# Alternating PSUM bank sets for the last down projection, and a sum of squares placed before its last quarter

## The reference

```python
h = rmsnorm(x, norm2_g[l])
u = causal_dwconv(jnp.einsum('bsd,df->bsf', h, ffn_up[l]), ffn_conv[l])
u_gate, u_val = jnp.split(u, 2, axis=-1)
x = x + jnp.einsum('bsf,fd->bsd', jax.nn.silu(u_gate) * u_val, ffn_down[l])
return rmsnorm(x, final_g)
```

## Time and profile before

| what | value |
|---|---|
| time, median of 3 executions | 2527.88 us |
| lowest and highest of the 3 | 2523.84 and 2528.88 us |
| profiled execution, its own time | 2525.59 us |
| profiled execution, its span (first to last instruction) | 2523.8 us |
| mean granted TensorE clock in it | 0.991 of full |
| TensorE busy with matmuls | 2456.4 us, 97% |
| VectorE busy | 1813.6 us, 72% |
| ScalarE busy | 1141.6 us, 45% |

### The profile page before, as it was taken

The page is one execution under the profiler, slowest core; times in us unless marked ns, Lnnn a source line. Parts: engine busy times, 40 slices in busy tenths (PEclk is TensorE's granted clock), DMA queues, the critical chain, the costliest instruction groups (busy, mean ns, idle before and its releaser), DMA issues.

```text
span 2523.8 us, 35020 instructions
## 1 busy us (share of the span) xinstructions
PE 2456.4 (97%) x13048; PEld 2062.8 (82%) x13048; DVE 1813.6 (72%) x2964; ACT 1141.6 (45%) x2080; POOL 0.3 (0%) x6
## 2 busy tenths in 40 slices
PE   8999999999998989999999999999999999999996
PEld 5888888777887657887888888888888888888884
DVE  6676666533344665338788888888888888888885
ACT  5444443323233444225555555555555555555542
POOL 0000000000000000000000000000000000000000
PEclk9999999999999989999999999999999999999998
DMA  4421112212325124213233333333333333333331
GB/s 170 151 71 52 69 54 71 83 64 108 109 85 210 42 100 151 94 61 120 89 101 101 101 103 112 109 106 110 102 102 108 101 101 101 105 101 101 101 121 67
DMA packets 72635, 252.82 MB, mean 100 GB/s; under 512 B 10112, under 2 KB 10240, under 8 KB 60716
## 3 DMA queue, kind: packets, MB, share of 16 engines
q1 hardware_dynamic: 72492, 250.91, 29.9%
HBM read 242.97 MB, written 13.15 MB: 101 GB/s over the span
## 4 chain that ended last, share of the span: by engine, by line
PE 54%; DVE 1%; issue 0%; ACT 0%; DVEq 0%; ACTq 0%
PE bank L1797 19%; PE bank L1778 15%; PE bank L1783 10%; PE bank L1758 4%; PE bank L1782 3%; PE bank L1781 3%; DVE x_t L2336 0%; DVE x_t L2327 0%; PE bank L2153 0%; DVE rms_row L2333 0%; ACT w_hi_far L1590 0%; DVE x_t L1957 0%; PE bank L2150 0%; PE bank L1765 0%; ACT rms_row L2255 0%
## 5 line engine op out<-in xcount | busy, mean ns | idle before, releaser
L1590 ACT ACTIVATE w_hi_far<-w_raw_far 128x512 fp32r<-128x512 f32 x768 | 484.1, 631 | 581.4 <-PE bank L1783 243.8
L1596 DVE TENSOR_TENSOR w_lo_far<-w_raw_far,w_hi_far 128x512 fp32r<-128x512 f32 x768 | 521.0, 688 | 165.2 <-ACT w_hi_far L1590 161.2
L1783 PE MATMUL bank<-y_parts,w_lo_far 128*128 128x256 f32 x2240 | 626.8, 280 | 0.0
L1778 PE MATMUL bank<-y_parts,w_hi_far 128*128 128x512 f32 x1600 | 565.8, 393 | 0.0
L233 PE MATMUL bank<-h_hi,w_hi 128*128 128x512 f32 x1120 | 471.7, 421 | 13.7 <-DVE w_lo L193 9.6
L1797 PE MATMUL bank<-ffn_g,w_hi_far 128*128 128x512 f32 x1408 | 466.9, 393 | 7.7 <-DVE x_t L2327 7.5
L233 PE MATMUL bank<-h_lo,w_hi 128*128 128x512 f32 x1120 | 440.6, 393 | 0.0
L233 PE MATMUL bank<-h_hi,w_lo 128*128 128x512 f32 x1120 | 439.8, 393 | 0.0
L1783 PEld LDWEIGHTS bank<-y_parts,w_lo_far 128*128 128x128 f32 x2240 | 421.6, 188 | 6.4
L1778 PEld LDWEIGHTS bank<-y_parts,w_hi_far 128*128 128x128 f32 x1600 | 300.4, 188 | 65.5
L193 DVE TENSOR_TENSOR w_lo<-w_raw,w_hi 128x512 fp32r<-128x512 f32 x312 | 203.7, 686 | 168.3 <-ACT w_hi L184 167.4
(11 more groups left out here) (309 smaller groups left out, 2657.6 us busy)
## 6 DMA issues: line engine op xcount, KB each, us to landing
w_raw_far<-in_ffn SPq DMA_DIRECT2D x167, 512.0 KB, 3.9
w_raw<-in_weights SPq DMA_DIRECT2D x77, 1024.0 KB, 5.0
w_raw_far<-in_ffn SPq DMA_DIRECT2D x162, 256.0 KB, 3.8
w_raw_far<-in_weights SPq DMA_DIRECT2D x8, 1024.0 KB, 4.9
x_t<-in_x_t SPq DMA_DIRECT2D x7, 1024.0 KB, 9.9
bias_rows<-bias_row SPq DMA_DIRECT2D x10, 512.0 KB, 7.5
mix_scratch<-head_out SPq DMA_DIRECT2D x14, 256.0 KB
out<-x_t SPq DMA_DIRECT2D x7, 512.0 KB, 2.7
```

What stands on the lines that cost most here:

```text
L1590: nc.scalar.activation(f_hi[:, act_q.n % FAR, :], src, ACT.Copy).then_inc(hi_done, 1)
L1596: nc.vector.tensor_tensor(f_lo[:, s, :], src, f_hi[:, s, :].bitcast(F32), ALU.subtract).then_inc(lo_done, 1)
L1778: nc.tensor.matmul(both, w_h, x.rearrange("p h n -> p (h n)"), start=new, stop=last, skip_group_check=True)
L1783: m = nc.tensor.matmul(main, w_l, x[:, 0, :], start=False, stop=last, skip_group_check=True)
```

## The change

The function for the last group is now `last_quarter_pe`. Chunks 0 and 2 write to `PB` in the order 0, 2, 3, 1, chunks 1 and 3 to `W`, and a chunk waits for the adds of the chunk two before it. Chunk 0 waits, bank by bank, for the readers of the last steps: ScalarE's copy of step 38 (bank 0), VectorE's corner sums of step 39 (banks 2 and 3), and ScalarE's last copy of step 39 (bank 1). Chunk 1 waits for the adds of step 39 from `W`. VectorE's adds read the bank that `last_bank` names. TensorE's product of `ssq` with ones (one matmul instruction in the text) stands before the last quarter of the last chunk instead of behind it, with its wait for the twelve summed squares. The lists of VectorE, ScalarE and the DMA queue are otherwise the same.

```diff
-            def down_quarter_pe(pe, st, group, kt, ends=False):
+            def down_quarter_pe(pe, st, group, kt):
...
-                    if ends and kt == GT - 1 and b < 3:
+                m.then_inc(q_used, 1)
+                pe_q.n += 1
+
+            def last_bank(c, b):
+                return PB[(0, 2, 3, 1)[b]] if c % 2 == 0 else W[b]
+
+            def last_quarter_pe(pe, c, kt):
+                s = pe_q.n % FAR
+                pe.wait_ge(lo_done, pe_q.at(1))
+                if c == 0:
+                    pe.wait_ge(gl_v, N_STEP + kt + 1)
+                x = g_tile(N_GROUP - 1, kt)
+                for b in range(4):
+                    if kt == 0:
+                        if c:
+                            pe.wait_ge(dn_free, 4 * N_STEP + 4 * (c - 1) + b + 1)
+                        elif b == 0:
+                            pe.wait_ge(cp_a, 6 + 5 * (N_STEP - 1))
+                        elif b < 3:
+                            pe.wait_ge(c_v, 3 * N_STEP + b)
+                        else:
+                            pe.wait_ge(cp_a, 6 + 5 * N_STEP)
+                    for n, (w, part) in enumerate(((f_hi, 0), (f_lo, 0), (f_hi, 1))):
+                        m = nc.tensor.matmul(last_bank(c, b)[:], w[:, s, b * P:(b + 1) * P], x[:, part, :],
+                                             start=(kt == 0 and n == 0), stop=(kt == GT - 1 and n == 2))
+                    if kt == GT - 1 and b < 3:
                         m.then_inc(dn_ps, 1)
...
                 for c in range(CG):
                     for kt in range(GT):
-                        down_quarter_pe(pe, Step(N_STEP + c), N_GROUP - 1, kt, True)
-                pe.wait_ge(ss_v, KT + 1 + SQ_SUMMED)
-                nc.tensor.matmul(PB[0][:], ones_f[:], ssq[:], start=True, stop=False)
+                        if (c, kt) == (CG - 1, GT - 1):
+                            pe.wait_ge(ss_v, KT + 1 + SQ_SUMMED)
+                            nc.tensor.matmul(PB[0][:], ones_f[:], ssq[:], start=True, stop=False)
+                        last_quarter_pe(pe, c, kt)
...
-                        nc.vector.tensor_tensor(dst, dst, W[b][:], ALU.add).then_inc(dn_free, 1)
+                        nc.vector.tensor_tensor(dst, dst, last_bank(c, b)[:], ALU.add).then_inc(dn_free, 1)
```

## The result

The changed kernel took 2512.60 us (median of 4 executions, 2511.55 to 2517.03) against 2526.49 us before (4 executions). The ratio is 0.9949, with a 95% interval of 0.9931 to 0.9966: faster by 0.5%, clear of noise, where 2515.0 in a range of 2511 to 2521 was forecast. A second set of five executions gave 2512.3 us and 0.9943 (0.9929 to 0.9956).

A forecast was written before the change was run, and what follows sets the result against it. It took TensorE's matmuls to bound the kernel (97% busy), with 12.43 us lost in the last group to late banks; that group falls from 56.23 to 45.36 us, gaining 11.7 to the root, hence 2515.0 us, range 2511 to 2521.

The forecast's parts named there:

- What bound the last group: Last group: banks emptied late by VectorE's adds behind a weight split, not late weights; 12.43 us lost of 56.23.
- Chunk 0: Last group's first chunk: start unmoved, no bank waits, fourth quarter stalls 0.65 us (0.5 to 1.0) for activations' tile 3.
- Chunks 1 and 2: Last group's middle chunks: no waits on banks, 10.95 us each (2.79 + 3 x 2.72).
- The moved product: `ssq` product before the last quarter: nothing won, its 0.86 us only shifts; twelfth sum's wait has 1.1 us spare; switch 0.05.
- The sum: New last group: 43.80 + 0.65 + 0.86 + 0.05 = 45.36 us; root 3.63 later; gain 11.7 us (11.2 to 12.0).
- The clock: TensorE's granted clock in the new last group: 1.00 throughout; the 12.43 us lost already contain the old half-clock loss.
- The wait for the twelfth sum: Rival, before the last quarter: new waits partly replace removed ones, likeliest here; 1 to 4 us lost, 2516 to 2519; chance 0.10.
- The weights as the bound: Rival, between chunks: 7 us of pauses stay, gain at most some 5, time 2521 to 2526; chance 0.05.
- going round more banks lowers the clock: Rival, last group: bank cycling drops TensorE to 1.2 GHz, matmuls 0.43 us instead of 0.227; chance 0.03.
- the slower rival: Whole last group at the lower clock adds 38 us, stated as 2541; chance 0.03.
- The total: Whole kernel: 2515.0 us, from the four executions' average 2526.55 and the gain of 11.7; range 2511 to 2521.
- a sign of being wrong that the time before the group moves by several us: Stretches before the last group should stay as they were; moving by several us by itself would make the prediction wrong.

The follow-up runs named there:

- adds_first: Kernel before, one set of banks, only VectorE's adds moved ahead of the low split of the next chunk's fourth quarter: group to root 49.07 us, ratio 0.9949.
- banks_only: Changed kernel with the `ssq` product back behind the last quarter, so only the two sets of banks: group to root 48.83 us, ratio 0.9941.
- sum_only: Kernel before with only the `ssq` product moved ahead of the last quarter: group to root 61.65, then 60.87 us, ratio 1.000.
- sum_earlier: Changed kernel with the `ssq` product one quarter earlier, before the last chunk's third quarter: group to root 50.74 us; one execution, 2516.57 us.
- bank_by_bank: Changed kernel, last chunk doing each bank's 12 matmuls in a row, fourteen squares summed on VectorE: group to root 47.22 us, median 2514.35, ratio 0.9950.

## Why the prediction was right

- **What bound the last group.** Right, and shown: it was the bank, not the weights. `adds_first` shows more than the prediction said. It named the order (TensorE ends a chunk, a quarter is split that isn't wanted yet, only then the adds) but treated more banks as what cures it; putting the adds before that split cures it as well, to 0.2 us.
- **Chunk 0.** Right. No wait on banks at its start; quarter 3 waits for the activations' tile. The sum had 0.65 us for this; it cost 0.82 (the fourth quarter begins 0.72 later than without a wait and takes 0.10 more).
- **Chunks 1 and 2.** No wait, as predicted. They took 10.88 us each against 10.95: a first quarter, priced at 2.79 us from one inside the loop, takes 2.72 like the others when no bank is late. The weights never were late.
- **The moved product.** Right that it is worth nothing (`banks_only`, `sum_only`); the twelfth sum ended 7.15 us after chunk 2, as in the prediction. Its spare time was 1.0 us against 1.1, and `sum_earlier` met the other side of that edge, with a pause of 1.61.
- **The sum.** 45.36 us to the last quarter's end were worked out, 45.24 measured; 48.99 to the root, 48.87 measured; the gain is 11.9 against 11.7. That the two agree to 0.12 us is in part luck, for two small errors had opposite signs: the four first quarters were 0.28 us too long in the sum, and the late tile 0.17 too short. The switch behind the product took 0.04, against 0.05.
- **The clock.** Right in the changed kernel: 1.00 throughout, as in all eight executions without the pauses at the chunks' ends. The prediction took the 12.43 us lost before as fixed; they are not. With the pauses the clock falls once or twice at places that change, and the group's length varies with it (60.72 and 61.03 us; 60.0 to 60.1 without a fall, by the chunks' times).
- **The rivals.** The wait for the twelfth sum didn't show. The weights as the bound are refuted by `adds_first`. That going round more banks lowers the clock found nothing for it: the group with eight banks held 1.00 and the one with four and its pauses didn't. By the Trainium skill ("TensorE: Matmul & The Clock Gate", "A second HAM failure mode: psum-queue depth-cycling") such cycling brought short idleness between the matmul groups of another kernel, and with it an oscillating clock. In the trace here the cycling brought no idleness between chunks and no fall; the falls came in the kernel whose TensorE did idle there. The prediction's price of the slower rival was added up wrongly: 38 us more on a forecast of 2515 is about 2553, not 2541. No run came near either.
- **The total.** 2515.0 was forecast and 2512.6 measured. The difference of 2.4 us is within what executions of one kernel differ by; whether a part of it is real stays open. The prediction also named as a sign of being wrong that the time before the group moves by several us. It did, by 3.27 us to the slower side in the profiled executions, but it lies inside the 6.6 us by which this start differs over all twelve.

## What to carry to other kernels

When TensorE pauses at a chunk's end, look at what stands ahead of the emptying instruction in its engine's list: here it was a weight split that TensorE itself released by ending the chunk, wanted only three quarters later, and a few lines of order were worth what a second set of banks was, to 0.2 us. Where executions differ by several us ahead of the place of interest, measure between two events around it: with a steady clock that length repeated to 0.02 us, and it told apart edits of 0.8 us. The medians here put `bank_by_bank`, shorter by 1.65 us, above the changed kernel.

## What the runs showed of the hardware

- TensorE's granted clock fell to its lower level, 0.50 (1.2 GHz), in the last group of each of the four profiled executions that had pauses of 2.13 us at the chunk ends, once or twice and in different chunks. Each of the six falls lies between 0.03 us before and 1.8 us after the end of such a pause (2489.77 in the execution of the earlier trace rows, after a pause to 2488.25), and six of the twelve pauses had none. In the group of the eight executions without those pauses it was 1.00, also with the one pause of 1.61 us in `sum_earlier`. That it is the pauses that bring it down is the nearest reading of this, not shown by a run that changes nothing else.
- VectorE's adds read one bank while TensorE wrote to another. The add below ran in chunk 1 of the changed kernel, which TensorE went through at 0.227 us a matmul. It took 0.68 us, as did one in the kernel before. No run here shows a price for it.

```profile
2463.35 0.68 DVE L2353 TENSOR_TENSOR x_t<-x_t,bank 128x512 f32<-128x512 f32 x1
```
